# One decoder layer on one core: four recurrence chunks side by side, a re-ordered router chain, the input projection in the tail, and a sample gather in two row groups

## The reference, cut to what matters

```python
def hgrn2_chunked(q, k, v, logf):            # prompt: chunks of 32 tokens, state S of each of 8 heads
    def chunk_step(S, xs):
        b = cumsum(lc); b_last = b[:, -1]
        qe = qc * exp(b);  ke = kc * exp(-b)
        scores = where(causal, qe @ ke.T, 0)
        o = qe @ S + scores @ vc
        S_new = exp(b_last) * S + (kc * exp(b_last - b)).T @ vc
        return S_new, o

h = rmsnorm(x, g_mix); z = h @ w_in          # q, f, i(v), g, u, gate_a, gate_b
o = rmsnorm(hgrn2(...), hg_norm) * silu(g)
x = x + (sigmoid(gate_a) * o + sigmoid(gate_b) * pool(u)) @ w_out
h = rmsnorm(x, g_ffn)
logits = h @ w_router + b_router             # 32 experts
top_v, top_i = top_k(logits, 4); top_w = softmax(top_v)
x = x + sum over the 4 experts of top_w * expert(h)
        # expert: gate = min(h@w_gate+b, 7); up = clip(h@w_up+b, -7, 7)
        #         ((up+1) * gate * sigmoid(1.702*gate)) @ w_down + b_down
x = x + sigmoid(rmsnorm(x, g_ple) @ w_ple_gate) * (p @ w_ple_proj)
y = rmsnorm(x, g_final)
```

## Time and profile before

| | |
|---|---|
| runs | 1386.6 us median (1386.1 to 1389.21) |
| profiled execution | 1386.59 us, of which the span of the trace is 1384.9 us |
| TensorE busy | 1331.2 us, 96% of the span |
| DVE, ACT, POOL busy | 332.9, 186.4, 68.3 us |
| moved by DMA | 458.70 MB, mean 331 GB/s |
| mean granted clock of TensorE | 0.982 |

### The profile page before, as it was taken

The page is one execution under the profiler, slowest core; times in us unless marked ns, Lnnn a source line. Parts: engine busy times, 40 slices in busy tenths (PEclk is TensorE's granted clock), DMA queues, the critical chain, the costliest instruction groups (busy, mean ns, idle before and its releaser), DMA issues.

```text
span 1384.9 us, 15843 instructions
## 1 busy us (share of the span) xinstructions
PE 1331.2 (96%) x6272; PEld 621.5 (45%) x6272; DVE 332.9 (24%) x633; ACT 186.4 (13%) x359; POOL 68.3 (5%) x145
## 2 busy tenths in 40 slices
PE   6999999999899999999999999999999999999995
PEld 5754557364434334343443434434344343434342
DVE  2423424122411221212212122121221212221133
ACT  3314311112111000110001000010000100100022
POOL 7021120030000000000000000000000000000000
PEclk9999999999789999999999999999999999999998
DMA  9743272252559999999999999999999999999920
GB/s 335 264 134 123 61 281 114 62 223 88 215 232 421 421 422 422 421 422 422 422 422 422 422 422 422 422 422 422 422 422 422 422 422 422 422 422 422 420 116 32
DMA packets 79264, 458.70 MB, mean 331 GB/s; under 512 B 8457, under 2 KB 9633, under 8 KB 30080
## 3 DMA queue, kind: packets, MB, share of 16 engines
q1 hardware_dynamic: 73376, 442.56, 77.9%
q0 software_dynamic: 4448, 14.98, 3.5%
q10 hardware_dynamic: 1408, 0.73, 0.2%
HBM read 452.35 MB, written 6.35 MB: 331 GB/s over the span
## 4 chain that ended last, share of the span: by engine, by line
PE 82%; DMA 10%; SPq 3%; DVE 3%; ACT 1%; issue 1%; POOL 0%; ACTq 0%; DVEq 0%
PE bank L965 39%; PE bank L629 10%; PE bank L930 10%; DMA arena<-in_w_up_dram 10%; PE bank L822 4%; PE bank L670 3%; PE bank L1006 3%; SPq L426 3%; PE bank L652 1%; PE bank L742 1%; PE bank L759 1%; PE bank L981 1%; DVE arena L1592 1%; PE bank L939 1%; PE bank L1010 1%; PE bank L598 1%
## 5 line engine op out<-in xcount | busy, mean ns | idle before, releaser
L965 PE MATMUL bank<-arena 128*64 128x512 f32 x3072 | 669.3, 594 | 12.1 <-DVE arena L1592 6.4
L965 PEld LDWEIGHTS bank<-arena 128*64 128x64 f32 x3072 | 226.2, 137 | 442.2 <-issue 438.3
L930 PE MATMUL bank<-arena 128*128 128x128 f32 (+1 forms) x816 | 157.3, 323 | 0.0
L629 PE MATMUL bank<-arena 128*128 128x512 f32 x320 | 144.2, 604 | 0.0
L930 PEld LDWEIGHTS bank<-arena 128*128 128x128 f32 (+1 forms) x816 | 120.6, 201 | 45.4 <-issue 18.0
L629 PEld LDWEIGHTS bank<-arena 128*128 128x128 f32 x320 | 59.8, 192 | 74.3 <-issue 73.5
L1600 DVE TENSOR_TENSOR arena<-bank,arena 128x512 f32<-128x512 f32 (+1 forms) x96 | 61.5, 682 | 96.3 <-PE bank L1006 96.1
L1578 DVE TENSOR_SCALAR arena<-bank 128x512 f32<-128x512 f32 x32 | 20.6, 686 | 195.4 <-PE bank L965 195.4
L1594 DVE COPY arena<-bank 128x512 f32<-128x512 f32 x16 | 11.1, 692 | 217.0 <-PE bank L965 217.0
L670 PE MATMUL bank<-arena 128*128 128x264 f32 x256 | 59.1, 395 | 3.2 <-DVE arena L1328 2.6
L1584 DVE TENSOR_SCALAR arena<-bank 128x512 f32<-128x512 f32 x32 | 20.6, 686 | 168.5 <-PE bank L965 168.5
(11 more groups left out here) (234 smaller groups left out, 736.9 us busy)
## 6 DMA issues: line engine op xcount, KB each, us to landing
arena<-in_w_gate_dram SPq DMA_DIRECT2D x128, 1024.0 KB, 25.5
arena<-in_w_up_dram SPq DMA_DIRECT2D x128, 1024.0 KB, 25.4
arena<-in_w_down_dram SPq DMA_DIRECT2D x128, 1024.0 KB, 21.4
arena<-in_w_in_dram SPq DMA_DIRECT2D x14, 2048.0 KB, 11.5
out_dram<-arena POOLq DMA_DIRECT2D x11, 512.0 KB, 3.8
arena<-in_state_hgrn_dram POOLq DMA_DIRECT2D x8, 512.0 KB, 14.8
arena<-in_w_out_dram SPq DMA_DIRECT2D x4, 1024.0 KB, 14.4
arena<-in_w_ple_gate_dram SPq DMA_DIRECT2D x4, 1024.0 KB, 26.3
```

What stands on the lines that cost most here:

```text
L629: ins = pe.matmul(job_bank(name)[:, :], hT[:, k, toks(t)], w[:, k, :], start=(k == 0), stop=(k == KD - 1))
L930: ins = pe.matmul(XG[c][:, (k % 4) * P:(k % 4 + 1) * P], h2[lanes(t), t, every_other(k)], oh[lanes(t), t, :], start=(t == 0), stop=(t == N ...
L965: ins = pe.matmul(out[c][hp(one), :], src[:, k * P + CAP * one:k * P + CAP * one + CAP], w[one][:, j, halves(c)], start=(first and k == 0) ...
```

## The change

- Recurrence: nine state buffers in place of two (where the samples' states lay, so DVE first waits until these are stored, and the loading of `w_out` now waits until the last `o` is filled and the prompt's state is stored). For each half of the heads of a token tile, the `dS` products of four chunks stand next to each other, each in its own 32 rows and its own bank; four such blocks alternate with `u` chunk steps. All `o` products follow at the end, those with the state taking four chunks in turn for each head. One `u` step of each chunk is left for after them.
- Router: logits are made tile by tile with tokens in the rows, the transposed form is gone, `b_router` is broadcast. All `h2T` copies but one are DVE's. The slot tables and the first selection come before the softmax weights. ACT loads the table of the exponential early. `gather` of the first pair is cut in pieces around `wT` and `bd`.
- The products `pp` with `w_ple_proj` go from the router stretch to the end of the expert loop; its weights, `g_ple` and `g_final` are now loaded by SP behind `w_ple_gate`, in ring places 4 and 5.
- Samples: their normalised rows are copied a second time into rows 32 to 39. The gather's sample products go last, in turns from row group 0 (bank 6) and row group 32 (bank 7). Within a pair the first gather half comes ahead of the turned selection matrix (now bank 7), and ACT copies the gathered rows after the expert output.
- Ring: places 8 to 11 now lie where `u`, `gb` and `dT` were and are freed by the turning of `mT` of tile 1.

The diff, cut to its core:

```diff
-    for n in range(NCH):
-        jobs.append((("dS", n, 0), 4, "v"))
-        jobs.append((("dS", n, 1), 7, "v"))
...
+    for t in range(2):
+        for half in range(2):
+            jobs += [(("dS", t, half, c), 4 + c, "v") for c in range(4)]
+    jobs += [(("o", t, half), 4 + 2 * t + half, "v") for t in range(2) for half in range(2)]
...
+            wait_filled(sp, ("o", 1, 1))
+            sp.wait_ge(s_stst, 16)
             for k in range(4):
                 sp.dma_start(wout[:, 2 * k:2 * k + 2], w_out[0]...
...
+            def load_ple(blocks):
+                used = NGRAN * NE * blocks + 1
                 for g in range(4):
+                    sp.wait_ge(s_used, used + g)
                     sp.dma_start(gran[g], ple[g]).then_inc(ld["ple"], 16)
+                sp.wait_ge(s_used, used + 4)
+                sp.dma_start(wproj, w_ple_proj[0].rearrange("(k p) n -> p k n", p=P)).then_inc(ld["wproj"], 16)
+                sp.wait_ge(s_used, used + 5)
+                sp.dma_start(gple_b, g_ple.partition_broadcast(P)[:, 0, :]).then_inc(ld["gple"], 16)
+                sp.dma_start(gfin_b, g_final.partition_broadcast(P)).then_inc(ld["gfin"], 16)
...
+            def state_steps(t, half):
+                for c in range(4):
+                    begin(("dS", t, half, c))
+                for j in range(4):
+                    hh = slice((4 * half + j) * P, (4 * half + j + 1) * P)
+                    for c in range(4):
+                        rr = slice(CH * c, CH * c + CH)
+                        ins = pe.matmul(job_bank(("dS", t, half, c))[:, j * P:(j + 1) * P], ktok[rr, t, hh],
+                                        v[rr, t, hh], start=True, stop=True)
+                        if j == 3:
+                            fill_done(ins, ("dS", t, half, c))
+            beside = [(n, k) for n in range(2) for k in range(KD - 1)]
+            for n in range(4):
+                state_steps(n // 2, n % 2)
+                for m, k in beside[4 * n:4 * n + 4]:
+                    chunk_step("u", m, k)
+            for t in range(2):
+                for half in range(2):
...
+                    for j in range(4):
+                        h = 4 * half + j
+                        for c in range(4):
+                            n = 4 * t + c
+                            if n > 0:
+                                ins = pe.matmul(job_bank(name)[CH * c:CH * c + CH, j * P:(j + 1) * P],
+                                                qh[:, h, n * CH:(n + 1) * CH], state[n][:, h, :], start=False, stop=True,
+                                                skip_group_check=True, tile_position=(0, CH * c))
+                    fill_done(ins, name)
+            for n in range(2):
+                chunk_step("u", n, KD - 1)
...
+            def logits(t):
+                for k in range(KD):
+                    for c in (0, 32)[:1 if t < 2 else 2]:
+                        ins = pe.matmul(job_bank(("lg",))[c:c + TS[t], t * NE:(t + 1) * NE], hT[:, k, toks(t)], wr[:, k, :],
+                                        start=(k == 0), stop=(k == KD - 1), skip_group_check=True)
+                return ins
...
+            def gather_samples():
+                for k in range(4):
+                    for c in range(2):
+                        rows = slice(32 * c, 32 * c + NS)
+                        ins = pe.matmul(XG[c][:, k * P:(k + 1) * P], h2[rows, 2, every_other(4 * c + k)], oh[rows, 2, :],
+                                        start=False, stop=True, skip_group_check=True, tile_position=(32 * c, 0))
+                        if k == 3:
+                            ins.then_inc(s_xg, 1)
...
+            gather(range(4))
+            turn_weights()
+            gather(range(4, 6))
+            down_biases()
+            gather(range(6, KD))
+            gather_samples()
...
-            keep_warm(8, Y[1])
+            pe.wait_ge(ld["wproj"], 16)
+            product("pp", 0, pT, wproj, 2)
             pe.wait_ge(s_end, 1)
+            product("pp", 1, pT, wproj, 2)
+            product("pp", 2, pT, wproj, 2)
             turn_rows("h3T", h3, lambda t: (s_rows, t + 7))
...
             squares(sq, 2)
+            for t in range(NT):
+                for n in pieces(t):
+                    copy_out(("pp", t, n), pps[t][lanes(t), cols(t, n)], piece(("pp", t, n)))
             turned("h3T", hT)
```

More of the change, by code:

```diff
@@ L755, in _ @@
-                    if n > 0:
-                        wait_drained(pe, ("dS", n - 1, 1))
-                        for j in range(4):
-                            h = 4 * half + j
-                            ins = pe.matmul(job_bank(name)[rr, j * P:(j + 1) * P], qh[:, h, n * CH:(n + 1) * CH],
-                                            state[n % 2][:, h, :], start=False, stop=True,
-                                            skip_group_check=True, tile_position=(0, row))
-                    if n % 4 == 3:
-                        fill_done(ins, name)
@@ new lines, in _ @@
+                    wait_drained(pe, ("dS", t, half, 3))
+                    for j in range(4):
+                        h = 4 * half + j
+                        for c in range(4):
[4 more added lines that the diff above has]
+                                                skip_group_check=True, tile_position=(0, CH * c))
@@ L901, in _, with turn_weights @@
-            fill_done(ins, ("wT",))
-            pe.wait_ge(ld["bdown"], 64)
-            wait_drained(pe, ("wT",))
-            for t in range(2):
+            keep_warm(2, bank[5])
+            def turn_weights():
+                pe.wait_ge(s_rt, 3)
+                begin(("wT",))
+                for t in range(NT):
+                    for r in range(4):
+                        ins = pe.matmul(bank[3][r * NE:(r + 1) * NE, toks(t)], wdn[lanes(t), t, :],
+                                        ident[lanes(t), lanes(t)], start=True, stop=True, tile_position=(0, r * NE))
+                fill_done(ins, ("wT",))
@@ new lines, in down_biases @@
+            def down_biases():
+                pe.wait_ge(ld["bdown"], 64)
+                wait_drained(pe, ("wT",))
+                for t in range(2):
+                    for half in range(2):
+                        name, rows = ("bd", t, half), slice((2 * t + half) * NE, (2 * t + half + 1) * NE)
+                        begin(name)
+                        fill_done(pe.matmul(job_bank(name)[:, :], wT[rows, toks(t)], bias_dd[rows, :], start=True,
+                                            stop=True, tile_position=(rows.start, 0)), name)
@@ L905, in _ @@
                 for half in range(2):
[L906 removed]
+                    name, rows = ("bd2", half), slice(half * NE, (half + 1) * NE)
                     begin(name)
[L908 to L914 removed]
@@ L1434, in _ @@
+            for t in range(2):
+                dve.wait_ge(s_ogp, t + 1)
+                for half in range(2):
+                    head_norm(("o", t, half), slice(0, P), t, half)
             flat, s = v[0:NS, 2, :], stat[32:32 + NS, 16:24]
```

325 lines of the change are left out of this document (128 added, 197 removed).

## The result

| | before | after |
|---|---|---|
| median on the same chip | 1386.6 us (1386.1 to 1389.21) | 1356.69 us (1355.74 to 1357.58) |
| span of the profiled execution | 1384.9 us | 1355.4 us |
| TensorE busy | 1331.2 us | 1253.1 us |
| mean granted clock | 0.982 | 0.988 |

The ratio is 0.9779, 95% interval 0.976 to 0.9798: 2.2% faster, 29.9 us by the medians. A fourth execution of the kernel before took 2835.38 us, twice the others, and is left out here. The forecast was 1353.9, which is 2.8 too low.

What follows compares the result with a forecast made beforehand. The loop was taken as a fixed DMA stream from the first freed ring place, so work saved before it counts in full; -12.3 - 20.0 - 1.7 + 1.3 = -32.7 from 1386.6 gave 1353.9 us, own range 1348 to 1359, overall 1346 to 1366.

Steps and rivals of the forecast that it cites:

- A: Recurrence, 96.6 us before: `dS` products in row groups and `o` products in column groups bring it to 84.3, -12.3.
- The waits of 3.1 and 1.8: Recurrence, ahead of gb: TensorE stands 3.1 us, does one product, stands another 1.8, as the first u banks' copies end late.
- The 4.4 for the `o` products: Recurrence: 56 `o` products with the state, in four groups of 32 columns, go from 13.0 to 4.4 us (bounds 3.2 and 13.0).
- Rivals 1 and 2: Recurrence: column groups gain nothing in `o`, +8.6 (chance 0.09); neither row nor column groups run side by side, another 10.4 (0.04).
- B: Router, from 343.30 to the first gate product at 392.05, 48.75 us before: that product comes at 372.1, -20.0.
- (b): Router: slot tables, no longer behind the softmax weights, start at 358.4 against 362.00; first selection ready at 359.6.
- The clock stays at 1.00: Router: two small `keep_warm` bursts leave no idle stretch over a microsecond, so the clock stays at 1.00; before it fell.
- Rival 3: Router: the clock falls all the same; gather, `wT`, `bd` double, +9, and C is lost, 1364.6; chance 0.10.
- C: First freed ring place: at full clock the issue comes 3.7 us after the first gate product instead of 5.4, -1.7.
- D: Last turn and tail: `pg` starts at 1339.7 against 1338.39, +1.3 (bounds -1 and +4).
- a tie: Tail: `w_ple_proj` lands at 1328.1, the same time as gather and spreading end, ahead of `pp`.
- Rivals 4 and 5: Expert loop: TensorE becomes its bound, say 1402.6 (chance 0.04); before it: transfers or a wait eat the earlier start, 1386 (0.05).

## Why the prediction was right, and where not

*What bounds the kernel*: right. Stream of 918 us from the first freed place, work in the turns free, work ahead of the loop counted in full. The run with 59 us more work in the turns shows it.

*A, -12.3, was -13.8*. The mechanism held. The blocks were 1.1 (start to start) where I took 1.35, the `o` part 8.3 where I took 8.5. The waits of 3.1 and 1.8 were 2.96 and 1.51, the clock's loss 1.8 was 1.6; a wait of 0.50 ahead of the first block I did not have. The 4.4 for the `o` products stands in the prediction without its working (13.0 at the rate of L829 gives 3.4), so that 4.3 came of them is in part luck. Rivals 1 and 2 are refuted: column groups with 32 columns run side by side as row groups do. By the rule that I cited from the Trainium skill ("TensorE: Matmul & The Clock Gate", Part 3) I had the 56 products stay at 13.0 us. The same part of the Trainium skill has a measured 2.38 times for three column groups with 32 columns of weights, which I passed over. Here the four rows make 4.3 us, and three groups run nearly three times as fast as one (24 records in 1.07 us, 8 records of one group in 1.06 before).

*B, -20.0, was -21.2*, by errors that cancel. (b) failed: the slot tables' order gave nothing, since the rank products came late. "The clock stays at 1.00" failed: it fell near 339.1, among the small logits products and one microsecond behind a wait of 0.87 us. The prediction asked only for waits under a microsecond, and that was not enough here. Rival 3 had the fall right but not its place: it was over when the gather began at 348.57, so 3 us were lost and not 9. The gather was quicker than I priced it: 16 records of it in 2.12 are 0.26 a product, not the 0.365 of a mean that held the samples' products. What was left is what leaves the path altogether: `pp` and its copies, and a gather at full clock.

*C, -1.7, was -1.7*; the issue 3.7 behind the first gate product, as forecast. That it came whole is luck. TensorE stands 1.14 us ahead of the first biases, a wait that the prediction does not weigh against the clock. In five of the twelve traces of the experiments the issue came 3.7 us behind the first gate product, in seven it came 4.9 to 5.4 behind, at a clock of 0.50 for some three microseconds.

*D, +1.3, was +5.3*: the mis-sized term, outside its bound of +4. (Its own pieces add up to 1339.4, not 1339.7.) The step "a tie" with the landing of `w_ple_proj` looked at the wrong thing: the weights landed 1.2 us behind the spreading, but with them landed nine microseconds ahead of need the hole stayed. The hole of 3.2 us goes with the loading of the code behind the branch, which no row of before shows as a wait, since there the load was over when the spreading ended. Behind the hole the clock fell, 2.8 us. Against these 6.0 stood 1.0 in the last turn (11.5 us from the landing to the end of the spreading, where I had 12.5) and 1.1 in `pp` and its sample rows (8.0 at full clock, where I had 9.1).

The errors are -1.5, -1.2, 0 and +4.0. With the front's scatter of +2.1, the stream's +0.3 and -0.4 behind `pg` they make up, within 0.1, the 3.2 us by which the span is longer than forecast. So the close total owes something to errors of both signs. Rivals 4 and 5 did not come: no turn is over 59.7, the stream has no hole.

Left open: why the instruction load comes 4 us ahead of the spreading's end in the kernel before and half a microsecond behind it after. The last expert input, for which the products ahead of the branch wait, is ready 3.5 us ahead of that end, before 4.0; that is half a microsecond of it. The trace of after also has a load of 8 KB on another instruction queue near 1290.5, of which that of before has none between 1320 and 1334. No run moved it alone. Open, too, is what decides whether the clock falls behind a wait of about one microsecond, at the loop's entry and among the logits.

## What to carry to other kernels

Before you call a time fixed, find the first event that the stream hangs on and price only what stands ahead of it. Small products in different 32-row or 32-column groups should take turns, innermost loop over the groups; the same products group by group give half of that or less. Behind a loop or over a skipped branch, put independent work ahead of the branch: in all three traces with that order the code's load was hidden, and the clock stayed. A clock that held behind a short wait in one trace need not hold in the next: look at several before you count it.

## What was not expected of the hardware

- Products of 128 x 32 weights in column groups: 32 records over four groups 1.08 us, 24 over three 1.07. Eight records of one group took 1.06 before: the other groups cost next to nothing on top.
- Four row groups in sequence within one block run at 2.79 us for 32 records, one group alone at 3.96, in turns at 1.17.
- The clock fell to 0.50 one microsecond behind a wait of 0.87 us among products of 32 columns (339.1 in the kernel after). Whether the wait or the small products do it, no run takes apart; filler in that wait put the fall off until behind the next wait, of 0.74 us.
- Behind a wait of some 1.1 us at the loop's entry (0.5 in one trace) it fell in seven of thirteen traces, behind the hole of 3.1 us in eight of ten, with hardly a difference in the work ahead.
- 2.8 us (2.75 to 2.92 by windows of 0.25) from the load of 16 KB of instructions to the next product, in all ten traces where TensorE waited for it.
